# Small mixers of the second block: merges cut into quarters of columns, short products in two row groups and two banks, latent attention moved nine rounds ahead

## What is computed

```
for l in range(2):
    h = rmsnorm(x, attn_norm_g[l])
    (cq, ckv, krope, cb, cc, cx, dq, dk, dv, iq, ik, iw,
     gq, gk, gv, glr, gr, gate_pre) = split(h @ w_in[l])
    o_mla  = mla_branch(...)        # latent attention, 4 heads of 96, causal
    o_conv = shortconv_branch(...)  # cb * conv3(cc * cx)
    o_dsa  = dsa_branch(...)        # 8 index heads of 32 score the keys, the top 64 are kept, 4 heads of 64 attend
    o_gla  = gla_branch(...)        # gated linear attention, 4 heads of 32 keys and 64 values
    gates = sigmoid(gate_pre)       # four gates of 1024
    merged = sum over n of gates[n] * (branches[n] @ w_branch[l, n])
    x = x + merged @ w_out[l]
    x = x + (silu(h2 @ w_ffn_gate[l]) * (h2 @ w_ffn_up[l])) @ w_ffn_down[l]   # h2 = rmsnorm(x)
```

## Time and profile before

| | before |
|---|---|
| median of 3 runs | 1969.67 us (1969.64 to 1970.01) |
| the profiled execution | 1969.93 us, span 1968.1 us |
| TensorE matmul busy | 1880.0 us (96%) |
| VectorE busy | 1243.8 us (63%) |
| ScalarE busy | 893.7 us (45%) |
| GpSimd busy | 233.7 us (12%) |
| mean granted TensorE clock | 0.965 of full speed |

### The profile page before, as it was taken

One profiled execution on the slowest core, in us unless ns is written; L12 is line 12 of the kernel. 1 busy time (PEld: TensorE's weight loads), 2 busy tenths in 40 slices (PEclk: granted clock), 3 DMA queues, 4 the chain that ended last, 5 costly groups with the idle time before them and its releaser, 6 DMA issues.

```text
span 1968.1 us, 30239 instructions
## 1 busy us (share of the span) xinstructions
PE 1880.0 (96%) x12540; PEld 1724.1 (88%) x12540; DVE 1243.8 (63%) x1744; ACT 893.7 (45%) x1226; POOL 233.7 (12%) x154
## 2 busy tenths in 40 slices
PE   8999968999999999999999989899999998989998
PEld 7998857998899887899887889899988888979996
DVE  5664896665566556566556855766645775586663
ACT  4443655444444445544444334454435433544442
POOL 0000541000000001000003333300001223330000
PEclk9999958999999998999999899999999999999999
DMA  7666412666566653466664334456655333446662
GB/s 235 187 183 192 142 54 72 185 180 195 171 184 170 203 186 109 127 184 175 200 185 129 107 97 132 145 171 184 186 185 166 107 108 107 143 150 183 182 191 98
DMA packets 241507, 309.60 MB, mean 157 GB/s; under 512 B 22158, under 2 KB 208686, under 8 KB 241370
## 3 DMA queue, kind: packets, MB, share of 16 engines
q1 hardware_dynamic: 241062, 306.57, 52.0%
q10 hardware_dynamic: 308, 1.09, 0.1%
HBM read 306.57 MB, written 1.05 MB: 156 GB/s over the span
## 4 chain that ended last, share of the span: by engine, by line
PE 74%; issue 12%; DVE 10%; ACT 2%; DMA 1%; POOL 1%; SPq 0%; DVEq 0%; POOLq 0%; ACTq 0%
PE ps L562 22%; PE ps L563 22%; PE ps L564 22%; DVE wlo L1538 2%; DVE ev_acc L1547 2%; PE ps L752 1%; PE ps L728 1%; PE ps L1008 1%; DVE m_scr L1547 1%; ACT whi L1100 1%; DVE m_G L1547 1%; PE ps L741 1%; DVE m_scr L2169 1%; PE ps L572 1%; DVE m_scr L2078 1%
## 5 line engine op out<-in xcount | busy, mean ns | idle before, releaser
L1538 DVE TENSOR_TENSOR wlo<-staging,whi 128x1024 fp32r<-128x1024 f32 (+2 forms) x523 | 668.6, 1285 | 494.3 <-ACT whi L1100 493.3
L562 PE MATMUL ps<-hTh,whi 128*128 128x256 f32 x2784 | 805.5, 289 | 16.2 <-POOL wlo L2292 7.6
L563 PE MATMUL ps<-hTl,whi 128*128 128x256 f32 x2784 | 797.2, 286 | 0.0
L564 PE MATMUL ps<-hTh,wlo 128*128 128x256 f32 x2784 | 796.6, 286 | 0.0
L1100 ACT ACTIVATE whi<-staging 128x1024 fp32r<-128x1024 f32 (+2 forms) x582 | 603.2, 1046 | 423.0 <-PE ps L564 415.7
L562 PEld LDWEIGHTS ps<-hTh,whi 128*128 128x128 f32 x2784 | 543.7, 195 | 25.3 <-issue 12.3
L563 PEld LDWEIGHTS ps<-hTl,whi 128*128 128x128 f32 x2784 | 544.2, 195 | 0.6 <-issue 0.5
L564 PEld LDWEIGHTS ps<-hTh,wlo 128*128 128x128 f32 x2784 | 544.0, 195 | 0.0
L562 PE MATMUL ps<-whi,fh 128*128 128x512 f32 (+1 forms) x528 | 209.5, 397 | 0.0
L563 PE MATMUL ps<-wlo,fh 128*128 128x512 f32 (+1 forms) x528 | 209.4, 397 | 0.0
L564 PE MATMUL ps<-whi,fl 128*128 128x512 f32 (+1 forms) x528 | 208.9, 396 | 0.0
(11 more groups left out here) (317 smaller groups left out, 1740.9 us busy)
## 6 DMA issues: line engine op xcount, KB each, us to landing
staging<-in_w_in SPq DMA_DIRECT2D x92, 512.0 KB, 3.7
staging<-in_ffn_w_down SPq DMA_DIRECT2D x88, 512.0 KB, 3.7
staging<-in_ffn_w_gate SPq DMA_DIRECT2D x84, 512.0 KB, 4.1
staging<-in_ffn_w_up SPq DMA_DIRECT2D x84, 512.0 KB, 4.0
staging<-in_w_ffn_gate SPq DMA_DIRECT2D x44, 512.0 KB, 4.1
staging<-in_w_ffn_up SPq DMA_DIRECT2D x44, 512.0 KB, 4.4
staging<-in_w_ffn_down SPq DMA_DIRECT2D x44, 512.0 KB, 3.3
staging<-in_od_w_in SPq DMA_DIRECT2D x16, 512.0 KB, 3.8
```

What stands on the lines that cost most here:

```text
L562: e.matmul(o, lh, rh, start=start, stop=False)
L563: e.matmul(o, lh, rl, start=False, stop=False)
L564: return e.matmul(o, ll, rh, start=False, stop=stop)
L1538: e.tensor_tensor(wlo[u % NH][:, 0:n], stage[u % NS][:, 0:n], whi[u % NH][:, 0:n].bitcast(F32), ALU.subtract).then_inc(*K.inc("lo", ("lo", ...
```

## The change

Five things, all in `mixer2` and in what it calls.

1. **Merges by quarters.** A unit of `w_branch` is now 256 rows by 256 columns (512 wide), one for each step of a merge. `FILL` ends gate 1, gate 3, merge 1, gate 2, merge 3, and then gate 0 and merge 2 quarter by quarter, merge 0 following from the third on. The last merge writes into `bh` and `bl`, where branches lie that have been merged. The merge units, the gate 0 units and the first unit of `down` leave GpSimd for VectorE.
2. **Levels.** The eight products of a level are issued as two halves with one wait between them; in each half two row groups write two banks.
3. **Index products.** Four products (two row groups, two banks) in a round, so two rounds instead of four for each half of the tokens. All later steps of `dsa` come two, then four rounds earlier.
4. **Scores of the `apart` attention.** Two banks, and no wait between the two.
5. **Latent attention.** It lies in `dsa`'s memory alone (its weights in the room of gate 0), starts in round 27, and its weights are loaded at unit 34 behind branch 1. `gla` has one more round ahead of its key transposes and two more ahead of its last transposes.

```
-FILL = [(1, False), (3, False), (1, True), (2, False), (0, False), (3, True), (2, True), (0, True)]
+    return (gates(1) + gates(3) + merges(1) + gates(2) + merges(3)
+            + [("gate", 0, 0), ("merge", (2, 0)), ("gate", 0, 1), ("merge", (2, 1)), ("gate", 0, 2),
+               ("merge", (2, 2), (0, 0)), ("gate", 0, 3), ("merge", (2, 3), (0, 1)), ("merge", (0, 2)),
+               ("merge", (0, 3))])
...
+            pooled.update(range(at + 12, len(plan), 2))
+                if kind == "gate":
+                    n, q = what
+                    if n:
+                        pooled.add(len(plan))
...
+                for n, q in what:
+                    plan.append(([(0, cols(A["w_branch_2"][l, n], 0, 2, 256 * q, 256 * q + 256), (2, 256))], 512))
-            pooled.update(range(at + 12, at + 64, 2))
...
 (attend, TensorE)
-                            if j and a.apart:
-                                e.wait_ge(*K.now("att"))
-                            w = e.matmul(ps[:, j * 256:j * 256 + nk], a.qT(h0 + j)[:, t * 128:t * 128 + 128],
+                            w = e.matmul(ps[j][:, 0:nk], a.qT(h0 + j)[:, t * 128:t * 128 + 128],
...
 (dsa, TensorE)
+                        for h0 in (0, 2):
+                            ps = room_pair((P, "idx", t, h0), (P, "idx", t, h0 + 1))
                             for j in range(2):
+                                for x in range(2):
+                                    rows = slice(32 * (h0 + x), 32 * (h0 + x) + 32)
...
 (gla, TensorE)
-                        for h in range(4):
+                        for half in range(2):
+                            if half:
+                                e.wait_ge(*K.at(P, "lev mm", lev, 0))
                             for t in range(2):
                                 sl = slice(t * 128, t * 128 + 128)
-                                if h:
-                                    e.wait_ge(*K.at(P, "lev mm", lev, h - 1, t))
+                                for x in range(2):
+                                    h = 2 * half + x
+                                    c = 256 * t + 128 * half
+                                    w = e.matmul(ps[x][:, c:c + 128], kk[32 * h:32 * h + 32, sl],
+                                                 qq[32 * h:32 * h + 32, sl], start=True, stop=True)
+                            w.then_inc(*K.inc("gla_mm", (P, "lev mm", lev, half)))
...
-                weave([(1, gates()), (14, short_conv()), (1, dsa()), (5, gla()), (36, mla())])
+                weave([(1, gates()), (14, short_conv()), (1, dsa()), (5, gla()), (27, mla())])
```

More of the change, by code:

```diff
@@ L502, in __init__ @@
                 self.uu = flat(self.G[:, 4:8, :])[:, 0:2 * (2 + S)].rearrange("p (a s) -> p a s", a=2)
[L503 removed]
+                self.place = [2, 6, 4, 0]
+                self.rows = [(self.bh[:, self.place[k // 2] + k % 2, :], self.bl[:, self.place[k // 2] + k % 2, :],
+                              everyrow, (P, "low", k // 2)) for k in range(8)]
             def N(self, a, b, t=None):
@@ L889, in gates @@
                         yield from tiles_in_turn(g, room((P, "cv", q)), (P, "cv mm", q))
[L890 to L902 removed]
+                    for kind, *what in FILL:
+                        if kind == "gate":
+                            q = 4 * what[0] + what[1]
+                            two_tiles = tiles_in_turn(g, room((P, "gate", q)), (P, "gate mm", q))
+                            next(two_tiles)
+                            yield
+                            next(two_tiles)
+                            done(P, "gate", q)
+                            yield
+                            continue
+                        for n, q in what:
+                            u, *w = unit()
+                            wh, wl = view(w[0], (2, 256)), view(w[1], (2, 256))
+                            if q == 0:
+                                e.wait_ge(*K.at(P, "branch", n))
@@ L975, in gla @@
                     done(P, "gup")
-                    for _ in range(5):
+                    for _ in range(6):
                         yield
@@ L1027, in gla @@
                         done(P, "go", t)
-                    for _ in range(6):
+                    for _ in range(8):
                         yield
@@ L2412, in gates @@
                         yield
-                    before = None
-                    for n, merge in FILL:
-                        if not merge:
-                            for q in range(4):
-                                yield
-                                side.due += 2
-                                yield
+                    for kind, *what in FILL:
+                        if kind == "gate":
+                            yield
+                            side.due += 2
+                            yield
                             continue
-                        for q in range(4):
+                        for n, q in what:
+                            side.due += 1
                             if n not in (0, 1) and q != 3:
```

247 lines of the change are left out of this document (117 added, 130 removed).

## The result

The changed kernel takes 1959.29 us (median; 1958.29 to 1960.95) against 1969.84 for the kernel before: the ratio is 0.9947, with a 95% interval of 0.993 to 0.9964. It is faster, but by 10.5 us and not by the 45 forecast, and lies outside the range. The profiled execution has a span of 1956.5 us, 11.6 less than before.

A forecast was written before the change was run, and what follows sets the result against it. TensorE was taken as the bound, matmuls busy for 96% of the span. Short products 11.9, waits 3.6 and clock 7 gave 22.5 us a mixer, 45 for two: 1969.9 to 1925 us, range 1897 to 1952.

The forecast's parts named there:

- The short products: TensorE's levels, index products and scores gain 5.7, 3.4 and 2.8 us, together 11.9 us a mixer.
- row groups don't run side by side: Rival: the 11.9 us on short products fall to about 0, giving 1949 us; chance 0.08.
- The stalls: TensorE's waits in a mixer: 18.7 us of old ones go, 15 of new ones come, gain 3.6.
- At the end: Start of `down`: of a 4.7 us wait perhaps 0.5 stays, for low parts of its first units on VectorE.
- At the states: First half of the state chain: TensorE waits about 1.2 us for VectorE, as before.
- In round 19: TensorE waits 5.5 us for weights that VectorE finishes last in round 16.
- The rotation: Round 34: TensorE waits 7.3 us a mixer, 4 if the norm finds gaps, 9 if another GpSimd unit falls in.
- The sentence on the search steps: VectorE's search steps have one input in SBUF and so would pass beside GpSimd, the 1 us end of the waiting.
- The clock: Of 14 us of full speed not granted around a mixer, 7 come back, between 2 and 10.
- VectorE sets the pace: Rival: from round 13 to 30 gains on short products are waited away; 1943 us, or 1950 with lower clock; chance 0.13.
- Bank pairs: Rival, rounds 17 to 24: banks taken in pairs make every round wait for VectorE's emptying; 2018 us, slower; chance 0.04.
- Small new waits: Rival: GpSimd out of step and norm in gaps, 12 us a mixer more gained; 1901 us; chance 0.17.

The follow-up runs named there:

- e4: Changed kernel with due weight conversions first: ahead of the tanh in gate 0 rounds, ahead of the merged rows' steps in merge 0 rounds; 1949.65 us.
- e3: Changed kernel with no low part of a weight unit on GpSimd in the two mixers, VectorE making all of them; 1942.41 us.
- e6: As e5, with index products, search and attention of the second half of the tokens two rounds later; 1921.67 us.
- e9: As e5, with ScalarE's due weight conversions ahead of the tanh in all gate rounds, not only gate 0; 1916.48 us.
- e8: Kernel before with only one edit: no low part on GpSimd in the mixers; 1936.63 us.
- e11: As e8, with GpSimd subtracting a buffer of its own from itself at the same 26 places a mixer, read by nobody; 1965.86 us.
- e5: Changed kernel with the edits of e3 and e4, and the latent attention started in round 34 in place of 27; 1922.42 us.
- e7: Kernel before with levels, index products and scores in paired row groups and banks, and no low part on GpSimd in the mixers; 1921.98 us.
- e10: As e7, with ScalarE's conversions ahead of the tanh in all gate rounds; 1922.01 us.
- e12: As e11, with one-input copies of 512 columns on GpSimd in place of the subtractions; 1946.21 us.

## Why the prediction was wrong

**The short products** were right, for the reason given. Levels came to 1.42 us against 1.45, and two products in two row groups start within 0.01 us of each other. The four steps of index products take 0.65, 0.71, 1.06 and 1.06, 3.5 against 3.4. The scores' own steps gave 2.4 of 2.8. The split has 10.4 of 11.9 us, less than these parts together, because other short products now stand at the low clock behind the new waits: the first state takes 1.12 us in place of 0.60, the first head transposes 1.59 in place of 0.83. The rival that row groups don't run side by side is out.

**The stalls** are where it failed: -3.6 was forecast, +9.3 measured, 12.9 us of the 16.5 missing in the first mixer. Of the 18.7 us of old waits nearly all went, as forecast; what failed is the sum of the new ones, 15 forecast and over 28 measured, a path on which I had counted VectorE's own work alone, without ScalarE's order ahead of it and without GpSimd holding it up. Term by term:

- *At the end*, 0.5 forecast, 5.8 measured, the worst single term. "VectorE owes multiply, add and the low part" counted VectorE's work and not ScalarE's order: conversions stood behind a tanh and behind the merged rows' high part. e4, which puts them first on both engines, removed 3.9 of the 5.8.
- *At the states*, 1.2 forecast as before, 5.4 measured. I had written that VectorE enters the stretch 5 us behind, and let TensorE feel it only in round 19. It felt it at once, at the first state, which needs a copy that VectorE makes behind the index sums. So the 3.4 us for the keys of `gla` did go, but a longer wait for VectorE stands 9 us further on. The collision is half of it: without GpSimd's units the wait is 2.5.
- *In round 19*, 5.5 forecast, 4.3 measured and 0.7 right behind it. The number was close by luck in part: TensorE waits there for a low part of GpSimd, not of VectorE as forecast, and the 4 us that I had put down to GpSimd's units did not go with them (6.1 in e3). e6 says that two rounds more for the search do not help, and e9 that 1.5 us are ScalarE's order.
- *The rotation*, 7.3 forecast, 9.2 measured, near the 9 that I had given if another of GpSimd's units falls into it, as it does. GpSimd stretches two steps there (2.36 us in place of 0.21, and 1.60 in place of 0.69 for one of the output gate ahead of it); but the 8.5 us of before held a stretched low part too (2.58 us in place of 1.22), which I had taken for VectorE's own work. Without GpSimd's units the wait is 6.5.
- *Beside them*, 3.3 us in small waits of 0.2 to 1.4, among them 1.1 for another low part of GpSimd; 0.3 forecast.

**GpSimd** is the failed step behind several of these: units beside VectorE were taken as free but for 4 us, and moving them as a cost. The prediction read in the earlier trace rows that low parts on VectorE take 1.82 us in the mixers and 1.285 in the whole program, added 4 us for three units in the stretch of the search, and went on: "the 8.5 low parts a mixer that go from GpSimd to VectorE cost it 1.15 each" (they were 9). e8 shows that going from GpSimd to VectorE is a gain: 52 such moves take 28 to 33 us off. The row had the answer: 29 low parts at 0.6 us over their price of 1.22 are 17 us a mixer of VectorE's time. The sentence on the search steps was right (e11), but what lay beside GpSimd's units were sums, rotation and low parts, which have two inputs.

**The clock** gave 4.9 us (about 2 in the second mixer) of the 7 forecast. The new waits leave stretches at the low clock behind them: in after, the 20 us around the wait for the rotation have a granted clock of 0.83.

```profile
1170.00:1190.00 20.00, 10.85 (x82) 10.57 (x81) 13.02 (x36) 4.28 (x6) 2.82 (x2) 0.83 0.26 79
```

**The rivals.** "VectorE sets the pace" had the right direction, that TensorE waits away what it gains, at 1943 to 1950. In the changed kernel it isn't a pace: e3, e4 and e5 remove waits with VectorE busy for as long (1233 to 1236 us). But e7 against e8 shows the rival's effect in part, as 4.4 us of a gain of 9.2 come back as waits. Bank pairs cost nothing that shows: 0.4 us of waiting for an eviction of scores, so the slower case (2018) is out. Small new waits (1901) missed by 58 us. Last, two runs of the kernel before were said to differ by less than 0.2%; over the later runs they differ by up to 0.4%.

## What to carry to other kernels

Before spreading work over a second elementwise engine, look for records of the first that are longer than their form's shortest, and try the kernel without the second: 26 subtractions of some 2.5 us a mixer on GpSimd cost 28 to 33 us here. Where a change shortens the rounds beside a chain (merge rounds of 1.43 us for gate rounds of 2.86), count each link of the chain against its own rounds, and move the whole chain, since moving one link moved the wait. In an in-order queue, try work that is ready ahead of work that waits for the current round's product: it brought 10 us in the last rounds (e4) and 6 in the others (e9), and nothing on the other base (e10). And time each part of a change by itself, since here one part brought 27 us and the others took 17 back, and time it again on each new base: the same part is worth 15 once GpSimd's units are gone.

## What the runs showed of the hardware

- GpSimd's subtraction and VectorE's two-input instructions in on-chip memory hold each other up, both ways: a rotation step took 2.36 us in place of 0.21, and GpSimd's pair 4.06 in place of 2.2. Work of GpSimd with no reader costs 29 us (e11), its copies 9.6 (e12).
- A `tensor_scalar` of VectorE with one tile and a constant is held as well (2.52 us in place of 0.43), while `max` and `match_replace` are not (0.42 and 0.41 us beside GpSimd, as without it).
- Eight products of 32 rows and 128 columns, in two row groups and two banks at once, with one wait between halves, take 1.42 us in place of 2.26 in two alternating chains of waits.
